# Attention: the two score halves of a tile around the value product of the tile in front, the transpositions last

## The reference

```python
def block(qs):
    a1, a2 = qs
    s1 = jnp.einsum('bqhd,bkhd->bhqk', a1, k1).astype(F32) * scale
    s2 = jnp.einsum('bqhd,bkhd->bhqk', a2, k2).astype(F32) * scale
    p = jax.nn.softmax(s1, axis=-1) - lam * jax.nn.softmax(s2, axis=-1)
    return jnp.einsum('bhqk,bkhe->bqhe', p.astype(v.dtype), v)

o = lax.map(block, (to_blocks(q1), to_blocks(q2)))
...
o = head_rmsnorm(diff_attention(q1, q2, K1, K2, V, lam), subln_g, post).reshape(B, L, DA_W)
y_lat = jnp.concatenate([o, fourier_mix(f)], axis=-1) @ w_out
```

## Time and profile before

| | |
|---|---|
| median of 3 runs | 4458.62 us (4455.81 to 4459.41) |
| span of the profiled execution | 4459.1 us |
| PE, PEld busy | 3904.5 us (88%), 3100.5 us (70%) |
| DVE, ACT busy | 2866.1 us (64%), 1920.4 us (43%) |
| attention and what is joined to it | about 236 to 388 us of the span |

### The profile page before, as it was taken

The page is one execution under the profiler, slowest core; times in us unless marked ns, Lnnn a source line. Parts: engine busy times, 40 slices in busy tenths (PEclk is TensorE's granted clock), DMA queues, the critical chain, the costliest instruction groups (busy, mean ns, idle before and its releaser), DMA issues. The chain is left out here.

```text
span 4459.1 us, 52231 instructions
## 1 busy us (share of the span) xinstructions
PE 3904.5 (88%) x18786; PEld 3100.5 (70%) x18786; DVE 2866.1 (64%) x3454; ACT 1920.4 (43%) x2313; POOL 883.7 (20%) x460
## 2 busy tenths in 40 slices
PE   6989898969888989788888888689999695999996
PEld 3756687737566777488888887468888473788885
DVE  4753776378657763444454455479998453899996
ACT  3041432233014322533333333267777222777774
POOL 0200000003100000122222221134554001355551
PEclk8989999979998999899999999889999897999998
DMA  5420354306412541100000001199998312999994
GB/s 193 151 96 21 115 186 151 110 28 215 153 38 95 175 165 58 28 20 19 18 7 13 19 19 38 40 356 360 356 369 308 132 58 79 384 369 361 365 360 154
DMA packets 372992, 689.31 MB, mean 155 GB/s; under 512 B 38979, under 2 KB 118979, under 8 KB 372228
## 3 DMA queue, kind: packets, MB, share of 16 engines
q1 hardware_dynamic: 328848, 641.88, 40.6%
q10 hardware_dynamic: 24724, 28.83, 1.9%
q0 software_dynamic: 19296, 16.94, 1.2%
HBM read 697.95 MB, written 41.00 MB: 166 GB/s over the span
## 5 line engine op out<-in xcount | busy, mean ns | idle before, releaser
L624 PE MATMUL psum<-work_rounded 128*128 128x512 f32 x3504 | 1164.4, 402 | 91.6 <-DVE work_rounded L618 31.1
L618 DVE TENSOR_TENSOR ring_rounded<-ring,work_rounded 128x2048 fp32r<-128x2048 f32 (+1 forms) x445 | 816.1, 1836 | 411.5 <-ACT work_rounded L613 279.6
L624 PEld LDWEIGHTS psum<-work_rounded 128*128 128x128 f32 x3504 | 666.9, 192 | 259.1 <-issue 112.0
L624 PE MATMUL psum<-work_rounded,fixed_rounded 128*128 128x512 f32 x2544 | 786.6, 403 | 31.5 <-POOL ring_rounded L618 10.2
L624 PE MATMUL psum<-work_rounded,ring_rounded 128*128 128x512 f32 (+1 forms) x1824 | 727.4, 399 | 0.0
L613 ACT ACTIVATE work_rounded<-ring 128x1024 fp32r<-128x1024 f32 x204 | 214.6, 1058 | 945.4 <-PE psum L624 689.6
L3176 ACT ACTIVATE work_rounded<-ring 128x2048 fp32r<-128x2048 f32 x256 | 490.7, 1918 | 264.5 <-PE psum L624 177.8
L624 PEld LDWEIGHTS psum<-work_rounded,fixed_rounded 128*128 128x128 f32 x2544 | 485.6, 191 | 151.3 <-issue 18.9
L624 PE MATMUL psum<-fixed_rounded,work_rounded 128*128 128x512 f32 (+1 forms) x1088 | 430.3, 395 | 0.0
L624 PEld LDWEIGHTS psum<-work_rounded,ring_rounded 128*128 128x128 f32 x1824 | 350.7, 192 | 81.2
L618 DVE TENSOR_TENSOR work_rounded<-work,work_rounded 128x2048 fp32r<-128x2048 f32 (+1 forms) x196 | 337.6, 1733 | 42.0 <-ACT work_rounded L3176 37.5
(11 more groups left out here) (348 smaller groups left out, 5839.9 us busy)
## 6 DMA issues: line engine op xcount, KB each, us to landing
ring<-in_w SPq DMA_DIRECT2D x128, 2048.0 KB, 12.1
work<-in_w SPq DMA_DIRECT2D x64, 2048.0 KB, 11.9
ring<-in_mod_w SPq DMA_DIRECT2D x24, 2048.0 KB, 8.9
ring<-in_ada_w SPq DMA_DIRECT2D x24, 2048.0 KB, 8.3
ring<-in_ffn_w_in SPq DMA_DIRECT2D x44, 1024.0 KB, 7.7
ring<-in_ffn_w_out SPq DMA_DIRECT2D x10, 2048.0 KB, 7.8
ring<-in_w_in_a SPq DMA_DIRECT2D x32, 512.0 KB, 6.0
ring<-in_hy_w_in SPq DMA_DIRECT2D x6, 2048.0 KB, 8.1
```

The source lines that it names most:

```text
L618: return eng.tensor_tensor(c.rounded(v), v, c.rounded(v_high), ALU.subtract)
L624: ins = pe.matmul(out, c.rounded(w), c.rounded(x), start=(start and i == 0), stop=(stop and i == 2))
```

## The change

PE's loop is put in another order. In turn i it issues `open_scores(i + 2)`, the value product of tile i - 1, `close_scores(i + 2)`, and then the transpositions of tile i; the value product of the last tile follows the loop. The value product becomes a function, `weigh_values`. ACT's result copy and square become `keep_out`, and stand one turn later: after the exponentials of tile i + 1 and before the copies of tile i, for tile i - 1. DVE's order is untouched, and so are all semaphores, their targets and every instruction's operands; no instruction is added or taken away.

```diff
         self.score_pair(pe, i, 0, True)
         self.score_pair(pe, i, 1, False).then_inc(self.scores, 1)
 
+    def weigh_values(self, pe, i):
+
+        c = self.c
+        h, t = i // NT, i % NT
+        pe.wait_ge(self.copied, i + 1)
+        for kt in range(NTA):
+            ins = pe.matmul(c.ps[:, 7, 256:256 + P], c.view(A_PT + T * kt + P * t, P),
+                            c.view(A_V + 512 * kt + P * h, P), start=(kt == 0), stop=(kt == NTA - 1))
+        ins.then_inc(self.out, 1)
+
+    def keep_out(self, act, i):
+
+        act.wait_ge(self.out, i + 1)
+        act.activation(self.raw[:, i, :], self.c.ps[:, 7, 256:256 + P], ACT.Copy).then_inc(self.kept, 1)
+        act.wait_ge(self.kept, i + 1)
+        act.activation(self.c.view(A_TMP, P), self.raw[:, i, :], ACT.Square, accum_out=self.ms[:, i:i + 1])
+
     def exponentials(self, act, i):
         act.wait_ge(self.negmax, i + 1)
         if i >= 2:
@@ -1028,9 +1045,12 @@
         self.close_scores(pe, 1)
         pe.wait_ge(self.lam_exp, 1)
         for i in range(self.TILES):
-            h, t = i // NT, i % NT
             if i + 2 < self.TILES:
                 self.open_scores(pe, i + 2)
+            if i:
+                self.weigh_values(pe, i - 1)
+            if i + 2 < self.TILES:
+                self.close_scores(pe, i + 2)
             pe.wait_ge(self.probs, i + 1)
             for kt in range(NTA):
                 if kt == 4 and i:
@@ -1038,13 +1058,7 @@
                 ins = pe.transpose(c.ps[:, 6 + kt // 4, P * (kt % 4):P * (kt % 4) + P],
                                    self.e(i, 0)[:, P * kt:P * kt + P], c.const("ident"))
             ins.then_inc(self.turned, 1)
-            if i + 2 < self.TILES:
-                self.close_scores(pe, i + 2)
-            pe.wait_ge(self.copied, i + 1)
-            for kt in range(NTA):
-                ins = pe.matmul(c.ps[:, 7, 256:256 + P], c.view(A_PT + T * kt + P * t, P),
-                                c.view(A_V + 512 * kt + P * h, P), start=(kt == 0), stop=(kt == NTA - 1))
-            ins.then_inc(self.out, 1)
+        self.weigh_values(pe, self.TILES - 1)
 
     def scalar(self, act):
         c = self.c
@@ -1058,15 +1072,14 @@
             t = i % NT
             if i + 1 < self.TILES:
                 self.exponentials(act, i + 1)
+            if i:
+                self.keep_out(act, i - 1)
             act.wait_ge(self.turned, i + 1)
             cols = slice(P * t, P * t + P)
             act.activation(pt[:, 0:4, cols], c.ps[:, 6, :].rearrange("p (k n) -> p k n", k=4), ACT.Copy)
             act.activation(pt[:, 4:6, cols], c.ps[:, 7, 0:256].rearrange("p (k n) -> p k n", k=2), ACT.Copy)
             act.drain().then_inc(self.copied, 1)
-            act.wait_ge(self.out, i + 1)
-            act.activation(self.raw[:, i, :], c.ps[:, 7, 256:256 + P], ACT.Copy).then_inc(self.kept, 1)
-            act.wait_ge(self.kept, i + 1)
-            act.activation(c.view(A_TMP, P), self.raw[:, i, :], ACT.Square, accum_out=self.ms[:, i:i + 1])
+        self.keep_out(act, self.TILES - 1)
         act.drain()
         act.activation(self.ms, self.ms, ACT.Sqrt, bias=c.eps(0), scale=1.0 / P).then_inc(self.std, 1)
 
```

## The result

| | before | after |
|---|---|---|
| median | 4457.78 us (4 runs, 4455.81 to 4459.41) | 4423.14 us (4 runs, 4419.29 to 4427.42) |
| span of the profiled execution | 4459.1 us | 4421.7 us |
| from the opening half of tile 2 to the last value product | 244.15 to 349.19: 105.04 us | 241.94 to 314.23: 72.29 us |
| from tile 1's transpositions to tile 14's | 88.23 us for 13 turns | 57.78 us for 13 turns |

The ratio is 0.9921, with a 95% interval of 0.991 to 0.9933: 34.6 us faster, where 4427 was forecast and 31.3 us of gain. The loop gives 105.04 - 72.29 = 32.75 us of the 37.4 us between the two profiled executions. Of the rest, 2.2 us lie ahead of the loop (its first row stands at 241.94 and not at 244.15) and 2.4 behind its last product, both in code that the change doesn't touch.

What follows compares the result with a forecast made beforehand. PE and DVE waiting for each other, plus low-clock turns, were taken to bound the attention loop. Its last product moving from 349.19 to 317.88 takes 31.3 us off 4459.1: 4427.8, by the median 4427.3; range 4422 to 4442.

Steps and rivals of the forecast that it cites:

- The circle: Attention loop before: PE and DVE wait for each other, transpositions 0.81 plus closing half to next transpositions 5.42: 6.23 us.
- PE's turn of 4.45 us: Changed loop at full clock: transpositions 0.81, score halves 1.05 each, value product 1.54, if nothing is waited for.
- The draws: Changed loop: copies take 1.86 us, covered by 1.86 of PE work; DVE's chain of 4.37 is 0.08 quicker than PE.
- The rival of turns of 5.0 us: Changed loop at full clock: near-equal waits each cost a tenth or two more, 7.7 us less gain, 4435; chance 0.15.
- ACT's room: ACT in its new order: 3.5 of 4.45 us used, 0.6 us spare ahead of copies and of the fifth transposition.
- The clock: Changed loop: almost no holes on PE, so granted clock 1.00 once it is there, from about 254 us.
- The second rival: Changed loop: the clock goes on swinging, turns of 5.53 us in the mean, 13 us less gain, 4440; chance 0.14.
- The start: Loop's beginning: low clock until about 253.0, tile 0's transpositions at 248.15, tile 1's at 254.85, a pair taking 2.00 us.
- The tail: Loop's end: tile 14's transpositions at 312.62, its product 1.86 later, tile 15 at 316.02, last product at 317.88.
- What follows shifts as a whole: Behind the loop: Fourier matmuls and all later stages move earlier unchanged, so the loop's 31.3 us is the whole gain.

Runs made afterwards that it cites:

- product_alone: Kernel before with the value product one tile late, ahead of the transpositions, and ACT's new order; closing half still behind the transpositions: 4457.99 us, ratio 0.9994.
- scores_alone: Kernel before with both score halves ahead of the transpositions; value product behind those of its own tile, ACT's order unchanged: 4442.74 us, ratio 0.996.
- block: Changed kernel with a tile's four score matmuls in one row ahead of the value product: 4418.08 us, ratio 0.991 against the kernel before.

## Why the prediction was right

- **The circle.** Transpositions, closing half, maxima, probabilities was named as the bound of before. `product_alone` left it closed and kept 6.23 us; `scores_alone` opened it. Right.
- **PE's turn of 4.45 us.** Measured 4.45, for twelve turns in a row. Its parts were 0.81, 1.05, 1.54, 1.05; measured 0.81, 1.06, 1.53, 1.05.
- **The draws.** The copies cost no wait of a matmul. Of DVE the text said that it would be the next bound, 0.08 us behind; the chain through the closing half is 4.37, as the step from tile 13 to 14 shows. But its own queue is 4.27, so that 0.18 us of work can be added before it costs anything. The rival of turns of 5.0 us is out.
- **ACT's room.** The text had 0.6 us ahead of the copies; the trace has 0.45. Ahead of the fifth transposition it has some 0.5.
- **The clock.** Taken at 1.00 in the loop; it is. The reason given, that the new turn has no holes, was tried from both sides: holes filled in the old order bring it to 1.00 (from 249 to 337 us), holes put into the new order bring back 0.79. The second rival is out with them. The Trainium skill's page "TensorE: Matmul & The Clock Gate", section "A second HAM failure mode: psum-queue depth-cycling", which stood behind that rival and tells it of bf16 matmuls of 512 columns, did not decide here: the loop changes PSUM banks with every group, and twelve turns ran at 1.00. They also did in `block`, where PE pauses 0.38 us ahead of each tile's transpositions.
- **The start.** This is the term that was mis-sized. The clock was let rise at 253.0, as in before, and tile 1 put 6.70 us behind tile 0. It was 5.12 us in one profile and 8.32 in the other, with the clock rising at about 247.5 and 256. The forecast is in the middle by luck; rows of one execution could not give it. The two halves of tile 2, which stand in a row there, take 4.14 us and not twice 2.00: the 0.14 was put at nothing. Had they no wait between them, the row would be shorter still: the four matmuls of `block` take 245.87 - 243.00 = 2.87 us there, most or all of it at the low level.
- **The tail.** Tile 14 to the last product: forecast 5.26, measured 5.25 (1.85, 1.45, 1.95; the last transpositions are 0.1 us longer, with a wait for the result copy in them, and the product in front is 0.1 shorter: two misses that cancel).
- **What follows shifts as a whole.** The Fourier matmuls take 41.26 us to the next stage's first one in before (350.63 to 391.89) and in after (315.67 to 356.93). Behind them it is within 1.4 to 2.4 us in the two profiles of after, though not in all kernels of the study; the text reckoned with no change there at all. The forecast of 4427 against 4423.14 rests on that too: the loop gave 29.5 to 32.75 us for the 31.3 forecast, and the rest of the 34.6 lies in code that nobody touched.

## What to carry to other kernels

Look for the circle that two engines close through each other, and ask which of its steps could be issued before the step that it now stands behind: here the closing half needed nothing of the transpositions, and only its place in a queue made DVE wait for them. Then put between two things that must follow each other something that is as long as the wait (the opening half over the copies, 1.06 us over 1.05). A hole on PE can be paid twice, once as idle time and once in low turns that follow: with holes of some 1.7 us in 6.2, 8.8 us of this loop went away with matmuls that compute nothing; a hole of 0.98 in 5.63 was paid only once. And look at what a wait in PE's queue separates: the same four score matmuls in the same order took 2.24 us with a wait in the middle and 1.49 with it ahead of the last.

## What was not expected

- At the loop's start a PE without gaps ran 12 us at a granted clock of 0.50 in one profile and 5.5 us in another, with the same instructions. In the loop each low stretch ended within a turn. The DMA was moving 381 GB/s at the start, but the first profile has 1.00 from 248 to 252 us beside 386 GB/s, so that alone doesn't hold the clock down. What sets the moment stays open.
- Float32 score matmuls on the two halves of the array's rows cost what the half with more columns costs, and about 0.2 us for each group: 256 and 512 columns take 1.06 us, 512, 512 and 256 take 1.48, 256 alone 0.62, and 256, 512, 512, 256 in one row 1.49. The same 1536 columns cost 2.1 us in two groups, in both divisions tried, 1.49 in one, and 2.24 in one with a wait in its middle.
- Code that no edit touched took 4094 to 4112 us in twelve profiles; in the one stage looked at, the granted clock differs with it.
